# A gather by quarters, an output projection by feature pairs, and a last expert quad by halves

## What is computed

```
def hierarchical_moe(h, ...):
    tok = h.reshape(b * t, d)
    ...                       # top-1 group of 8 experts, top-2 experts in it, combine weights
    for e in range(N_EXPERTS):
        y = (jax.nn.silu(tok @ expert_gate[e]) * (tok @ expert_up[e])) @ expert_down[e]
        out = out + combine[:, e:e + 1] * y.astype(jnp.float32)
    return out.astype(h.dtype).reshape(b, t, d)
```

## Time and profile before

| | us |
|---|---|
| median of 3 runs (lowest, highest) | 819.71 (818.97, 821.42) |
| the profiled execution, its own time | 816.45 |
| its span, from the first to the last instruction | 814.7 |
| PE busy | 778.4 (96% of the span) |
| DVE busy | 314.2 |
| ACT busy | 204.3 |
| moved by DMA | 254.02 MB, mean 312 GB/s |

### The profile page before, as it was taken

How to read it: one execution, slowest core, us unless ns; L and a number is a source line. 1 busy time by engine, 2 the same in 40 slices (tenths; PEclk the granted TensorE clock), 3 DMA queues, 4 the chain that set the end, 5 groups by cost and what they waited for, 6 DMA issues and landing times.

```text
span 814.7 us, 16557 instructions
## 1 busy us (share of the span) xinstructions
PE 778.4 (96%) x6516; PEld 550.1 (68%) x6516; DVE 314.2 (39%) x751; ACT 204.3 (25%) x432; POOL 3.3 (0%) x11
## 2 busy tenths in 40 slices
PE   8999999999999998899999999999999999999976
PEld 7876888878855554465588768888787555554523
DVE  4757243762612111111277563446635111111102
ACT  2443541531410000000214545326212000001003
POOL 1000000000000000000000000000000000000000
PEclk9999999999999999899999999999999999999989
DMA  9952264594999999999996332665949999999995
GB/s 348 418 182 84 99 226 160 158 367 156 379 422 420 419 421 420 421 422 420 418 415 237 130 104 66 221 194 187 366 191 399 422 422 419 422 420 420 420 422 238
DMA packets 41641, 254.02 MB, mean 312 GB/s; under 512 B 4833, under 2 KB 9825, under 8 KB 12769
## 3 DMA queue, kind: packets, MB, share of 16 engines
q1 hardware_dynamic: 40992, 252.22, 77.8%
q10 hardware_dynamic: 576, 0.81, 0.3%
HBM read 250.52 MB, written 1.44 MB: 309 GB/s over the span
## 4 chain that ended last, share of the span: by engine, by line
PE 64%; DMA 14%; DVE 14%; issue 3%; ACT 3%; DVEq 1%; SPq 0%; ACTq 0%; POOLq 0%
DMA ring<-e_down 14%; PE ps L1082 12%; PE ps L623 9%; PE ps L1051 6%; PE ps L960 6%; PE ps L1103 6%; DVE xn L1467 3%; PE ps L1111 3%; PE ps L1115 3%; PE ps L795 3%; PE ps L852 2%; PE ps L821 2%; DVE space L1590 2%; PE ps L652 2%; PE ps L885 1%
## 5 line engine op out<-in xcount | busy, mean ns | idle before, releaser
L623 PE MATMUL ps<-hT,ring 128*128 128x256 f32 x800 | 183.4, 382 | 0.0
L623 PEld LDWEIGHTS ps<-hT,ring 128*128 128x128 f32 x800 | 148.5, 190 | 22.9 <-issue 3.5
L1051 PEld LDWEIGHTS ps<-hT,xn 128*128 128x128 f32 x640 | 73.0, 192 | 9.5 <-issue 7.4
L1051 PE MATMUL ps<-hT,xn 128*128 128x128 f32 x640 | 76.8, 278 | 1.9 <-DVE hT L1816 1.9
L1082 PE MATMUL ps<-space,hT 128*32 128x256 f32 x992 | 64.6, 404 | 9.4 <-DMA space<-e_up 5.7
L1103 PE MATMUL ps<-ring,space 128*32 128x512 f32 x456 | 55.2, 598 | 9.0 <-ACT space L1408 7.6
L960 PE MATMUL ps<-xn,ring 128*128 128x256 f32 x256 | 57.8, 381 | 0.0
L1082 PEld LDWEIGHTS ps<-space,hT 128*32 128x32 f32 x992 | 30.8, 114 | 39.0 <-DMA space<-e_up 11.5
L1816 DVE TENSOR_TENSOR hT<-shapes,sel 128x128 f32<-128x128 f32 x40 | 9.9, 288 | 112.2 <-PE ps L1089 111.9
L960 PEld LDWEIGHTS ps<-xn,ring 128*128 128x128 f32 x256 | 48.1, 190 | 7.2 <-issue 0.7
L1885 DVE COPY hT<-ps 128x512 f32<-128x512 f32 x18 | 12.4, 691 | 90.3 <-PE ps L1103 90.3
(11 more groups left out here) (295 smaller groups left out, 916.8 us busy)
## 6 DMA issues: line engine op xcount, KB each, us to landing
ring<-e_down SPq DMA_DIRECT2D x50, 1024.0 KB, 26.7
ring<-e_up SPq DMA_DIRECT2D x36, 1024.0 KB, 15.4
ring<-w_mix SPq DMA_DIRECT2D x33, 1024.0 KB, 9.5
space<-e_up SPq DMA_DIRECT2D x26, 1024.0 KB, 26.2
space<-e_gate SPq DMA_DIRECT2D x24, 1024.0 KB, 19.5
more_buf<-e_gate SPq DMA_DIRECT2D x14, 1024.0 KB, 10.8
ring<-e_gate SPq DMA_DIRECT2D x8, 1024.0 KB, 8.1
ring<-w_mix SPq DMA_DIRECT2D x14, 512.0 KB, 16.1
```

The costliest lines, as they stand in the source:

```text
L623: mm = pe.matmul(bank, slot_w(i)[:, k, ct * P:(ct + 1) * P], hT3[:, k, :], start=(k == 0), stop=(k == KD - 1))
L1051: mm = pe.matmul(ps[:, 4 + 3 * half_, kk * P:(kk + 1) * P], xn3[:, j, k * P:(k + 1) * P], Psel[:, j, :], start=(j == 0), stop=(j == TT - 1))
```

## The change

Five things are done:
1. `w_out` is laid out by pairs of input tiles: slot k holds tiles 2k and 2k+1 for all outputs, so slots are freed while the projection runs (`weights_read`): the first after tile 3 of group 0, the second and `L` after tile 4 of group 0, the third after tile 6 of group 0, the fourth at the end. `L` moves ahead of the last two slots in the list of `expert_slots`.
2. `gather` goes by quarters. Quarters 0 and 1 of the next round are made where the whole was; quarters 2 and 3 are made in the round itself, after the first and the second gate slot. DVE copies quarters (`selected`). `Psel` and `Pwt` become one buffer: `weigh` moves to the start of the round, behind the copies of quarters 2 and 3. The wait for the sums to be set moves from before the first round to before its first scatter.
3. In the last quad of both layers both parts of `scatter(0, ...)` come before the second feature half, which is done by halves of 256 features into two PSUM banks (`down_half`), each copied and scattered by itself. In layer 0 `scatter_half` is the old `scatter(1, part)`; in layer 1 it does both token tiles for 256 features.
4. The last load of a layer (m = 95) goes as two transfers of half the bytes, and its bytes are reordered to match.
5. In the last quad of layer 1, four matmuls of ones (`keep_busy`, IDLE = 4) follow each of the first three up slots and the first `down`; nothing reads their result.

The diff, without new semaphores, renumbered waits and the host's reordering of `w_out`:

```diff
@@ -118,7 +119,7 @@
-return ["N0", "N1"] + ring[0:8] + ["C", "D", "S0", "S1", "K2", "S3", "S2", "K"] + ring[8:12] + ["L", "Y", "X"]
+return ["N0", "N1"] + ring[0:8] + ["C", "D", "S0", "S1", "K2", "S3", "S2", "K"] + ring[8:10] + ["L"] + ring[10:12] + ["Y", "X"]
@@ -326,8 +327,8 @@
-Psel = ysb[:, 0, 256:512].rearrange("p (t s) -> p t s", t=TT)
-Pwt = kq[:, 768:1024].rearrange("p (t s) -> p t s", t=TT)
+Psel = kq[:, 768:1024].rearrange("p (t s) -> p t s", t=TT)
+Pwt = Psel
 PwT = kq[:, 1024:1280]
@@ -533,8 +538,12 @@
             sync.wait_ge(freed[need[0]], need[1])
-        src = (e_gate, e_up, e_down)[m % 12 // 4]
-        sync.dma_start(slot[b], src[l, 4 * (m // 12) + m % 4]).then_inc(arrived[b], 16)
+        src = (e_gate, e_up, e_down)[m % 12 // 4][l, 4 * (m // 12) + m % 4]
+        if m + 1 < NMOE:
+            sync.dma_start(slot[b], src).then_inc(arrived[b], 16)
+        else:
+            sync.dma_start(slot[b][:, 0:SLOT // 2], src[:, 0:SLOT // 2]).then_inc(arrived[b], 16)
+            sync.dma_start(slot[b][:, SLOT // 2:SLOT], src[:, SLOT // 2:SLOT]).then_inc(last_half, 16)
 sync.wait_ge(moe_freed, last_use[gain_slot][1])
@@ -953,13 +962,21 @@
     b = bank_of[("wo", n)][0]
-    w = slot_w(NPROJ + n)
     for k in ks:
+        have_slot(NPROJ + k // 2)
+        w = slot[loads[l][NPROJ + k // 2][0]][:, k % 2 * D + n * COLS:k % 2 * D + (n + 1) * COLS]
         for i in range(2):
-            mm = pe.matmul(ps[:, b, i * T:(i + 1) * T], w[:, k, i * P:(i + 1) * P], mixT[:, k, :],
+            mm = pe.matmul(ps[:, b, i * T:(i + 1) * T], w[:, i * P:(i + 1) * P], mixT[:, k, :],
                            start=(k == 0 and i == 0), stop=(k == KD - 1 and i == 1), skip_group_check=True)
+    if n == D // COLS - 1 and ks[-1] in (3, 5):
+        mm.then_inc(wo_read, 1)
     return mm
+def weights_read(turn, n):
+    pe.wait_ge(wo_read, upto(l, wo_read, turn))
+    pe.sem_inc(mix_freed, n)
@@ -982,28 +998,31 @@
 head_norm(5, msq[:, 0, :])
-begin_out(1)
+begin_out(1).then_inc(wo_read, 1)
 pe.wait_ge(mix_ready, upto(l, mix_ready, GP + RP))
...
     project_out(n, [3])
+    if n == 0:
+        weights_read(1, 1)
 head_norm(7, msq[:, 2, :])
...
     project_out(n, [4])
+    if n == 0:
+        weights_read(2, 2)
 pe.wait_ge(mix_ready, upto(l, mix_ready, 6))
...
     project_out(n, [6])
+    if n == 0:
+        weights_read(3, 1)
 pe.wait_ge(mix_ready, upto(l, mix_ready, 8))
...
     done(project_out(n, [7]), ("wo", n))
-for n in range(D // COLS):
-    b, u = bank_of[("wo", n)]
-    pe.wait_ge(full[b], upto(l, full[b], u + 1))
-    pe.sem_inc(mix_freed, 1 if n + 1 < D // COLS else 2)
+buffers_read(("wo", D // COLS - 1), 1)
@@ -1041,20 +1060,24 @@
-def gather(n):
-    pe.wait_ge(psel_ready, n * 2 + 1)
-    for half_ in range(2):
...
+def gather(part):
+    for kk in range(2):
+        k = 2 * part + kk
+        c0 = part // 2 * T + kk * P
+        for j in range(TT):
+            mm = pe.matmul(ps[:, 4 + 3 * (part % 2), c0:c0 + P], xn3[:, j, k * P:(k + 1) * P], Psel[:, j, :],
+                           start=(j == 0), stop=(j == TT - 1))
+    mm.then_inc(gath_full, 1)
+def gather_ahead(n):
+    pe.wait_ge(psel_ready, n * 2 + l + 1)
+    gather(0)
+    gather(1)
 pe.wait_ge(xn_ready, upto(l, xn_ready, 2))
-gather(rounds_done(pe, rounds) + l)
-pe.wait_ge(sums_set, upto(l, sums_set, 4))
+gather_ahead(rounds_done(pe, rounds))
 b = bank_of["rank"][0]
@@ -1068,28 +1091,40 @@
+at_end = q + 1 == QUADS
+def keep_busy(count):
+    if at_end and l + 1 == LAYERS:
+        for _ in range(count):
+            pe.matmul(ps[:, 7, T:T + P], ones[:, :], ones[:, :], start=True, stop=True)
...
             w = slot_of(4 * m + i)
-            if m == 0 and i % 2 == 0:
-                pe.wait_ge(hq_ready, (n + l) * 2 + i // 2 + 1)
+            if m == 0:
+                pe.wait_ge(hq_ready, n * 4 + 2 * l + i + 1)
             for k in (2 * i, 2 * i + 1):
...
             mm.then_inc(slot_done, 1)
+            if m == 0 and i < 2:
+                gather(i + 2)
+            elif m == 1 and i < 3:
+                keep_busy(IDLE)
...
     pe.wait_ge(pwt_ready, n + 1)
-    gather(n + l + 1)
+    gather_ahead(n + 1)
@@ -1103,6 +1138,32 @@
+def down_half(f, part):
+    w = slot_of(10 + f)
+    if f and part:
+        pe.wait_ge(last_half, 16 * (l + 1))
+    for e in range(4):
+        c0 = part * SLOT // 2 + e * 256 if f else e * 512 + part * 256
+        mm = pe.matmul(ps[32 * e:32 * e + 32, 6 + part, 0:256], hmT[:, f, 32 * e:32 * e + 32],
+                       w[:, c0:c0 + 256], start=(f == 0), stop=(f == 1), skip_group_check=True)
+    if part:
+        mm.then_inc(slot_done, 1)
+    elif f:
+        mm.then_inc(down_first[l], 1)
+def scatter_half(part):
+    if l + 1 < LAYERS:
+        scatter(1, part)
+        return
+    c0 = part * 256
+    for j in (1, 0):
+        mm = pe.matmul(ps[:, 2 * j + 1, c0:c0 + 256], PwT[:, j * P:(j + 1) * P], ysb[:, 1, c0:c0 + 256],
+                       start=False, stop=False, skip_group_check=True)
+        if part:
+            mm.then_inc(sums, 1)
@@ -1117,15 +1178,33 @@
 down(0, 0)
+if at_end:
+    pe.wait_ge(hq_ready, n * 4 + 2 * l + 6)
+keep_busy(IDLE)
 down(0, 1)
-down(1, 0)
-pe.wait_ge(y0_ready, n + 1)
-scatter(0, 0)
-down(1, 1)
-scatter(0, 1)
-pe.wait_ge(y1_ready, n + 1)
-scatter(1, 0)
-scatter(1, 1)
+if not at_end:
+    down(1, 0)
+    pe.wait_ge(y0_ready, n + 1)
+    if q == 0:
+        pe.wait_ge(sums_set, upto(l, sums_set, 4))
+    scatter(0, 0)
+    down(1, 1)
+    scatter(0, 1)
+    pe.wait_ge(y1_ready, n + 1)
+    scatter(1, 0)
+    scatter(1, 1)
+else:
+    pe.wait_ge(y0_ready, n + 1)
+    scatter(0, 0)
+    scatter(0, 1)
+    down_half(0, 0)
+    down_half(0, 1)
+    down_half(1, 0)
+    down_half(1, 1)
+    pe.wait_ge(y1_first[l], r + 1)
+    scatter_half(0)
+    pe.wait_ge(y1_ready, n + 1)
+    scatter_half(1)
 pe.reg_add(rounds, rounds, 1)
@@ -1819,22 +1898,23 @@
-def selected(n, halves=range(2)):
-    for half in halves:
-        dve.wait_ge(gath_full, n * 2 + half + 1)
-        TTn(hq[:, half * 4:half * 4 + 4, :], ps[:, 4 + 3 * half, :].rearrange("p (k s) -> p k s", k=4),
-            gq[:, half * 4:half * 4 + 4].unsqueeze(2).to_broadcast([P, 4, P]), ALU.mult).then_inc(hq_ready, 1)
+def selected(n, parts):
+    for part in parts:
+        dve.wait_ge(gath_full, n * 4 + 2 * l + part + 1)
+        c0 = part // 2 * T
+        TTn(hq[:, part * 2:part * 2 + 2, :], ps[:, 4 + 3 * (part % 2), c0:c0 + T].rearrange("p (k s) -> p k s", k=2),
+            gq[:, part * 2:part * 2 + 2].unsqueeze(2).to_broadcast([P, 2, P]), ALU.mult).then_inc(hq_ready, 1)
@@ -1845,44 +1925,49 @@
 dve.sem_inc(routed, 1)
+selected(n0, [0])
 link(dve.tensor_scalar(nmore[:, :], nround_f[:, QUADS:2 * QUADS], -1.0, 0.0, ALU.add, ALU.max))
 dve.sem_inc(more_ready, 1)
+selected(n0, [1])
 link(experts(2, 0))
 link(experts(3, 1))
-selected(n0, [0])
 dve.wait_ge(route_exp, upto(l, route_exp, 1))
...
 link(dve.reciprocal(rt[:, :, 62:63], rt[:, :, 61:62]))
-selected(n0, [1])
 link(TTn(rt[:, :, 52:53], rt[:, :, 62:63], rt[:, :, 29:30], ALU.mult))
...
 link(TTn(sel[:, 1, :, 0:EXPERTS], pick[:, 1, :, :], pick[:, 3, :, :], ALU.add))
-weigh(slice(0, 4), n0)
...
         n = rounds_done(dve, rounds)
+        selected(n, [2, 3])
+        weigh(slice(q * 4, q * 4 + 4), n)
         dve.wait_ge(pwt_full, n + 1)
         with dve.If(r < nv - 1):
-            select(slice(q * 4, q * 4 + 4), iota[:, bass.ds(r * CAP + CAP + 1, CAP)], n + l + 1)
-            weigh(slice(q * 4, q * 4 + 4), n + l + 1)
+            select(slice(q * 4, q * 4 + 4), iota[:, bass.ds(r * CAP + CAP + 1, CAP)])
         with dve.Else():
-            select(slice(q * 4 + 4, q * 4 + 8), iota[:, 1:1 + CAP], n + l + 1)
-            weigh(slice(q * 4 + 4, q * 4 + 8), n + l + 1)
+            select(slice(q * 4 + 4, q * 4 + 8), iota[:, 1:1 + CAP])
         dve.wait_ge(sg_ready, n + 1)
...
         TTn(hmid, sg, ps[:, 6, 0:DE], ALU.mult).then_inc(hmid_ready, 1)
-        selected(n + l + 1)
-        dve.wait_ge(slot_done, n * QSLOTS + 12)
-        dve.tensor_copy(ysb[:, 1, :], ps[:, 6, :]).then_inc(y1_ready, 1)
+        selected(n + 1, [0, 1])
+        if q + 1 == QUADS:
+            dve.wait_ge(down_first[l], r + 1)
+            dve.tensor_copy(ysb[:, 1, 0:256], ps[:, 6, 0:256]).then_inc(y1_first[l], 1)
+            dve.wait_ge(slot_done, n * QSLOTS + 12)
+            dve.tensor_copy(ysb[:, 1, 256:512], ps[:, 7, 0:256]).then_inc(y1_ready, 1)
+        else:
+            dve.wait_ge(slot_done, n * QSLOTS + 12)
+            dve.tensor_copy(ysb[:, 1, :], ps[:, 6, :]).then_inc(y1_ready, 1)
         dve.reg_add(rounds, rounds, 1)
@@ -1971,7 +2056,9 @@
 down = features_by_tile(g["expert_down"]).reshape(LAYERS, QUADS, 4, P, 2, 2, 512).transpose(0, 1, 5, 4, 3, 2, 6)
-experts = [rows_by_slot(g["expert_gate"]), rows_by_slot(g["expert_up"]), down.reshape(LAYERS, EXPERTS, P, SLOT)]
+down = down.reshape(LAYERS, EXPERTS, P, SLOT)
```

(11 more changed lines are left out.)

19 lines of the change are left out of this document (6 added, 13 removed).

## The result

| | before | after |
|---|---|---|
| median of the timed runs, same chip (number of runs) | 819.53 us (22) | 823.68 us (22) |
| lowest, highest | 816.85, 822.24 | 816.77, 826.12 |
| the profiled execution, its own time and span | 816.45, 814.7 | 825.82, 823.9 |
| its mean granted clock | 0.987 | 0.985 |

The ratio is 1.0038, with a 95% interval of 1.0020 to 1.0055: the change costs 3.1 us, 1.6 to 4.5. It is not the ratio of the two medians, which lie 4.15 apart: 13 of the changed kernel's 22 runs crowd between 823.5 and 826.2, the rest reach down to 816.8, and the means are 3.0 apart. The forecast was +1.4. Its range, 817.6 to 823.7, held the time by 0.02 us, which is luck.

What follows compares the result with a forecast made beforehand. While the experts run DMA is full and PE nearly so, about 8 us behind. Layer 0's +1.9 and layer 1's -0.5 sum to +1.4 on a median of 819.71, giving 821.1 us, range 817.6 to 823.7.

Steps and rivals of the forecast that it cites:

- Part 1: Output projection, w_out slots freed early: gain of 0 in layer 0 and 0.6 us in layer 1.
- The hole: Ten us of idle DMA, 193 to 203, before w_out's slots are freed; forecast to move in front of Y.
- "ten idle us" rival: The idle DMA time ahead of w_out's freed slots is won: about 804 us, chance 0.05.
- Part 2: Gather by quarters in expert rounds: rounds begin 1.84 us earlier, but four more block changes cost 0.5 us a round.
- The new waits: Gate slots 2 and 3 waiting for DVE's copies of quarters: hidden, by 0.2 us only.
- rival of free block changes: Changes between gate and gather blocks cost nothing: layer 0 loses 0.4, layer 1 gains 0.8, 819.3 us; chance 0.20.
- Part 3: Last quad of layer 0, reordered: layer 1 starts 1.9 us later, 0.4 plus 1.5.
- D: Start of the first down in layer 0's last quad: forecast 400.6, with layer 1's first projection 8.5 us after it.
- Part 4: Layer 1's last quad: transfers still pace it, and ACT's square comes 0.5 us earlier.
- slower rival: PE becomes the bound in layer 1's last quad, from 0.63 us a round; 823.5 us at 0.8; chance 0.22.
- Sum: Layer 0's +1.9 and layer 1's -0.5 give +1.4 us, 821.1 us against the median.
- the clock stood in the text as a gain: Rival: ones prevent a low-clock stretch in layer 1's tail, 817.8 us, chance 0.09.

Runs made afterwards that it cites:

- kernels 2: Kernel before with the gather by quarters alone, old w_out layout and old last quad, no ones: 821.32 us, ratio 1.0021.
- kernels 6: Changed kernel with the last quad and last load as they were, no ones: 820.75 us, ratio 1.0024.
- kernel 5: Kernel before with the reordered last quad of both layers and the halved last load, gather by halves, no ones: 821.80 us, ratio 1.0046.
- 8: Kernel before with the new last quad, early w_out slots, and the unread gather after each layer's last round left out: 820.28 us, ratio 1.0026.
- kernel 10: Kernel before with ones added in layer 0's sixth quad and layer 1's last quad, where PE waits for loads: 823.82 us, ratio 1.0049.
- 11: 8 with ones in layer 0's sixth quad, the scores' wait and layer 1's last quad: 820.23 us, ratio 1.0006.
- 12: 11 with the sixth quad's ones in its first round only and the unread gather left out in layer 0 alone: 819.59 us, ratio 1.0000.
- kernel 7: Kernel before with the new last quad and the unread gather after each layer's last round left out: 822.45 us, ratio 1.0056.

## Why the prediction was right or wrong

**Part 1: right, the size in part by luck.** The hole moved in front of `Y`; gains of 0.1 and 0.57 for 0 and 0.6. In layer 1 the load came 1.55 sooner in the one trace, and the clock took about 1 of it back. The "ten idle us" rival is out.

**Part 2: right in kind, mis-sized.** "0.12 to 0.13 each, 0.5 us a round" measured 0.165 and 0.66. The trace of before had given 0.15 per block; I had shaved it with no row behind me. The measured value lies inside the bounds that were given, 0 and 0.2. The new waits were hidden, as said: no row of PE between gate slots has a wait. The rival of free block changes is refuted for these two tile shapes. The Trainium skill ("TensorE: Matmul & The Clock Gate", section "Step-by-step: what each phase is for") has the next weights load under the present matmul; within a block the rows agree (0.86 a slot), but a change of tile costs 0.165 all the same. What in the change takes that time no row shows.

**Part 3: right.** The working from D (8.5) measured 8.45. D came 1.96 later for 1.5, which is three rounds of 0.66. Together +2.31 for +1.9. What the text did not see: with PE later by the quarters the old order would have found its last load landed and needed 7.48 after D (kernels 2 and 6), so that the new one costs 0.97 there and not 0.4.

**Part 4: the end right, the bound wrong.** "The transfers still pace it", with 1.2 us to spare over 9 rounds and a threshold of 0.63 us a round. The rounds took 0.66, so PE was the bound, as the slower rival had it. Its price was over-stated: 0.03 above the threshold costs little (PE comes to the fourth up slot 0.06 behind its load), and ACT's square (817.35 in the row below) stands 190.45 behind the layer's first gather, where before it stood 191.03 behind (808.08 less the cut, 617.05): 0.58 earlier, for a forecast of 0.5. What Part 1 gained is in this.

```profile
817.35 0.60 ACT L1499 ACTIVATE xn<-ps 128x512 f32<-128x512 f32 x1 [2.85 <-PE ps L1163]
```

**Sum: +1.4 forecast, +1.66 in the traces' expert stages, +3.1 (1.6 to 4.5) in the timed runs.** The step that failed is the sum's silent term: the mixing stages were taken as unchanged, and the clock stood in the text as a gain, and as a loss only in the up slots of layer 1's last quad. They took 5.7 us more in the trace, with 6.8 lost. The kernel before takes two of its stretches at 1.2 GHz inside waits for loads. The quarters and the ones fill those of layer 1 with work, so a stretch at the low clock falls more often on work that sets the end, at up to 0.82 us for each lost. That this fills the gap of 1.4 us is what the two slopes, the table of mixing stages and the count over 14 traces suggest, not something I have shown: the interval also reaches down to 1.6, the part that is accounted for, and only one execution of each kernel was profiled. Why the changed kernel had two stretches in mixing and the kernel before none in its one trace stays open. Kernels without quarters (5, 8, 10, 11, 12) had some too, and two of these (5, 8) had no ones either, so it is neither as such.

The forecast of the class, no difference that could be told, came out. That the time fell into the range is luck: the terms of the sum account for 1.66, and the rest came from a term that was not in it.

## What to carry to other kernels

Count the changes of tile shape that an interleaving adds, and price each by the rows (here 0.165 us); finer pieces pay only where they cover more than that. Before you make an engine busier in a stretch that waits for loads, ask what that slack was absorbing: here it seems to have hidden over half of the clock's losses (the kernel before paid 0.35 of 0.82). For differences under half a per cent compare stages, and note the clock lost in each, before you believe a median.

## What the runs showed of the hardware

- A change between 128*32 products and 128*128 ones costs 0.165 us, the mean of ways in and out: 20.32 to 20.35 for 19.67 us in every one of the changed kernel's 15 undisturbed rounds, with four more changes.
- Less work on PE did not mean less time: kernel 7, with 32 gather records fewer per layer than kernel 5, ran at a mean clock of 0.978 for 0.983 and took 822.45 for 821.80 us.
- In kernel 10, with products of ones in the waits for loads, the granted clock was 1.00 where before had 0.57 (326 to 334 and 786 to 794), without a gain in time. A stretch at the low clock in such waits was nearly free: 192.22 for 192.16 us with 3.4 us lost (kernels 6 and 2).
- The clock also halved where PE was hardly idle: at 618, at the end of 32 records of 40 columns (616 to 618: busy 2.00 of 2.00).
- A one-core kernel can start at the low clock or not: the first projection's 24 records took 5.42 us in seven traces and 6.84 to 7.18 in the other seven, and the trace's clock record need not show it.
